# Leaving out the constant matmuls that TensorE runs inside the gaps of the norms

## The reference

```python
def _layernorm(x, g=None, b=None):
    xc = xf - jnp.mean(xf, -1, keepdims=True)
    y = xc * lax.rsqrt(jnp.mean(xc * xc, -1, keepdims=True) + NORM_EPS)

# first stack: a context stream (ctx) and a latent stream (x), two layers
#   mixer: attention + gated linear attention + 31-tap convolution, gated, times w_out
xc = _post(xc, yc, ...);  xc = _post(xc, _ffn(_modulate(xc, ...), p), ...)
x  = _post(x, _latent_mixer(...), ...);  x = _post(x, _ffn(_modulate(x, ...), p), ...)
# _ffn: (silu(h @ w_gate) * (h @ w_up)) @ w_down, inner width 2816

# second stack: latent attention, short convolution, pooling, sliding-window attention
h = rmsnorm(x, attn_norm[l]);  proj = h @ w_in[l]
gf = groups * lax.rsqrt(jnp.mean(groups * groups, axis=-1, keepdims=True) + RMS_EPS)
x = x + mixed @ w_o[l]
h2 = rmsnorm(x, ffn_norm[l])
x = x + (jax.nn.silu(gate) * up) @ w_down[l]
```

## Time and profile before

| | |
|---|---|
| runs | 3501.25, 3501.73, 3507.51 us |
| profiled execution, first to last instruction | 3497.9 us, its own time; 3.8 us under the median of the runs |
| TensorE matmul busy | 2956.0 us, 85% |
| VectorE | 2445.7 us, 70% |
| GpSimd | 2045.3 us, 58% |
| ScalarE | 1542.4 us, 44% |
| mean granted TensorE clock | 0.913 of full speed |
| DMA | 441.59 MB, mean 126 GB/s |

### The profile page before, as it was taken

One profiled execution on the slowest core, in us unless ns is written; L12 is line 12 of the kernel. 1 busy time (PEld: TensorE's weight loads), 2 busy tenths in 40 slices (PEclk: granted clock), 3 DMA queues, 4 the chain that ended last, 5 costly groups with the idle time before them and its releaser, 6 DMA issues.

```text
span 3497.9 us, 57524 instructions
## 1 busy us (share of the span) xinstructions
PE 2956.0 (85%) x21332; PEld 2740.1 (78%) x21332; DVE 2445.7 (70%) x2987; ACT 1542.4 (44%) x2508; POOL 2045.3 (58%) x823
## 2 busy tenths in 40 slices
PE   6866968889975897788998768977889989998998
PEld 5755968789974687777997756876889878997898
DVE  3978684776698858767664898676676665656565
ACT  4324544444541444434445323444354454445444
POOL 6735643658763565455874543644568545874587
PEclk7977989999987998989998979989899999999999
DMA  6424422435441343333542221322355423542354
GB/s 208 137 72 133 145 73 85 151 122 175 156 133 61 109 134 111 105 109 113 176 168 97 99 95 61 130 99 97 121 178 175 132 97 108 175 162 97 110 178 163
DMA packets 121571, 441.59 MB, mean 126 GB/s; under 512 B 13552, under 2 KB 15600, under 8 KB 120992
## 3 DMA queue, kind: packets, MB, share of 16 engines
q1 hardware_dynamic: 121088, 435.30, 37.3%
q10 hardware_dynamic: 288, 3.47, 0.2%
HBM read 437.67 MB, written 1.05 MB: 125 GB/s over the span
## 4 chain that ended last, share of the span: by engine, by line
issue 58%; POOL 38%; PE 2%; POOLq 1%; DVE 0%; ACT 0%; DVEq 0%; ACTq 0%
POOL w_lo L417 38%; PE lin L458 1%; PE lin L460 1%; PE lin L459 1%; POOLq L413 1%; POOLq L416 0%; POOLq L417 0%; DVE arena L2067 0%; DVE s_lo L1559 0%; DVE rstd L1499 0%; PE aux L565 0%; DVE rstd L1496 0%; DVE tmp L1498 0%; DVE y_buf L1597 0%; ACT w_hi L984 0%
## 5 line engine op out<-in xcount | busy, mean ns | idle before, releaser
L417 POOL TENSOR_TENSOR w_lo<-w_raw,w_hi 128x1024 fp32r<-128x1024 f32 x819 | 2045.1, 2503 | 1444.6 <-ACT w_hi L984 1440.6
L458 PE MATMUL lin<-h_hi,w_hi 128*128 128x256 f32 x3584 | 1041.0, 290 | 84.0 <-POOL w_lo L417 67.7
L459 PE MATMUL lin<-h_lo,w_hi 128*128 128x256 f32 x3584 | 1028.4, 287 | 0.0
L460 PE MATMUL lin<-h_hi,w_lo 128*128 128x256 f32 x3584 | 1027.5, 287 | 0.0
L984 ACT ACTIVATE w_hi<-w_raw 128x1024 fp32r<-128x1024 f32 x819 | 861.5, 1052 | 189.8 <-PE lin L458 113.2
L458 PEld LDWEIGHTS lin<-h_hi,w_hi 128*128 128x128 f32 x3584 | 702.7, 196 | 98.4 <-issue 64.0
L459 PEld LDWEIGHTS lin<-h_lo,w_hi 128*128 128x128 f32 x3584 | 703.2, 196 | 0.6
L460 PEld LDWEIGHTS lin<-h_hi,w_lo 128*128 128x128 f32 x3584 | 702.1, 196 | 0.0
L1621 DVE SCALAR_TENSOR_TENSOR arena<-arena,vec 128x256 f32<-128x256 f32 x720 | 517.6, 791 | 0.0
L458 PE MATMUL lin<-s_hi,w_hi 128*128 128x256 f32 x1584 | 467.4, 295 | 58.5 <-DVE s_lo L1559 23.3
L459 PE MATMUL lin<-s_lo,w_hi 128*128 128x256 f32 x1584 | 461.1, 291 | 0.0
(11 more groups left out here) (241 smaller groups left out, 4372.5 us busy)
## 6 DMA issues: line engine op xcount, KB each, us to landing
w_raw<-in_stream SPq DMA_DIRECT2D x819, 512.0 KB, 3.3
X<-in_tokens SPq DMA_DIRECT2D x2, 1024.0 KB, 10.5
arena<-in_const ACTq DMA_DIRECT2D x1, 1856.0 KB, 7.8
arena<-in_small ACTq DMA_DIRECT2D x1, 1536.0 KB, 11.2
out<-arena SPq DMA_DIRECT2D x1, 1024.0 KB, 3.9
arena<-in_masks SPq DMA_DIRECT2D x1, 960.0 KB, 12.0
const<-in_const SPq DMA_DIRECT2D x1, 690.0 KB, 7.3
wglr<-in_w_glr SPq DMA_DIRECT2D x1, 384.0 KB, 9.7
```

The costliest lines, as they stand in the source:

```text
L417: pool.tensor_tensor(w_lo[:, s, :], w_raw[:, s, :], w_hi[:, s, :].bitcast(F32), ALU.subtract).then_inc(sems["lo_ready"], 1)
L458: used(pe.matmul(o, whi, hi[:, k, :], start=k == 0, stop=False), first)
L459: pe.matmul(o, whi, lo[:, k, :], start=False, stop=False)
L460: mm = pe.matmul(o, wlo, hi[:, k, :], start=False, stop=k == kcs - 1)
```

## The change

The function, its constant and its five calls are removed. Nothing else is added or moved.

```diff
-IDLE = 10
...
-            def keep_clock(k):
-                for _ in range(k):
-                    pe.matmul(aux[3][:, 0:S], c1("mean1024"), const1[:, 0:S], start=True, stop=True)
...
                     layernorm(x, "x_ready")
                     unit(l, s, ("adt", beside[1][1]))
-                    keep_clock(IDLE)
                     n.up("h_ready", KC)
                     feed_forward()
                     if turn == 3:
                         pe.wait_ge(sems["sum_ready"], n.at("sum_ready"))
                         sum_to_mean()
                         variance(M)
-                        keep_clock(IDLE)
...
             for l in range(DEPTH):
                 variance(M)
-                keep_clock(IDLE)
                 ready = "h_ready", n.at("h_ready")
                 n.up("h_ready", KC)
                 dense_together(2, ready)
...
                 head_rows([("head256", c // 2, M[:, c, :]) for c in range(KC)])
-                keep_clock(IDLE // 2)
                 pe.wait_ge(sems["row_ready"], at.up("row_ready"))
...
                 variance(M)
-                keep_clock(IDLE)
                 n.up("h_ready", KC)
                 feed_forward()
```

## The result

The changed kernel takes 3517.16 us (median of five, 3510.05 to 3517.40) against 3501.25 us before (five, 3499.26 to 3507.51): 15.9 us slower, ratio 1.0041, interval 1.0029 to 1.0054. A second set of five runs (experiment 5) gave 3515.67 us and 1.0049 (1.0036 to 1.0063). The profiled execution has a span of 3515.4 us; 3515.9 had been worked out. The mean granted clock went from 0.913 to 0.907.

The account below looks back on a forecast made before the run. TensorE was taken to bound the long projections, so delays there count. Clock falls of 14.0 us before projections, 1.2 behind L873 and 2.8 ahead of `spread_row` summed to 18.0 us, giving 3520 us, range 3508 to 3531.

Parts of the forecast that it names:

- What bounds: Long projections: TensorE bounds, 185 of 190 us busy against GpSimd's 159 in the first feed-forward; its losses there reach the kernel.
- The removed matmuls are worth nothing: In the norm gaps, the 180 fill records, some 41 us of TensorE, are covered by the VectorE chain; removal brings 0 directly.
- A fall in every gap: Without fill, the granted clock was expected to fall in each gap of this change, 3.7 to 6.5 us long.
- 2.0 us for each of seven places: Seven places leading into projections: the half clock behind each gap costs 2.0 us, 14.0 us together; ends 8.4 and 21.
- The Trainium skill's half of the throttled time: Rule pricing a clock fall at half the throttled time: 2.6 us for a place before projections, 18 us for seven.
- L873, 1.2 us: Behind L873, the last eight `variance` records run at half clock: 1.2 us taken, 1.4 us at most, 0 at least.
- The two ahead of the spread, 1.4 each: Two places ahead of `spread_row`: the clock falls before the eight L590 records, 1.4 us each, together 2.8; ends 0 and 3.7 each.
- Sum: Whole kernel: 14.0 + 1.2 + 2.8 = 18.0 us slower, so 3515.9 us in a profile and 3520 us as median.
- (a): Rival, deep falls: the clock stays low 10 us or more at most places, +26 to +35 us, 3528 to 3537; chance 0.12.
- (b): Rival, no measurable loss: late, short falls at all seven projection places, 6 us or less, at most 3508; chance 0.09, shared.
- (c): Rival: fill at half clock ends late, so removal wins 1.6 us at such places; 3492 with all eight; chance 0.03.
- (d): Rival: the clock does not go by what TensorE does, so only noise is left, 3502; shares a chance of 0.09.

Follow-up runs that it names:

- experiment 5: The changed kernel, all ten fills out, timed again with no edit: 3515.67 us, 1.0049 against the kernel before.
- experiment 6: The kernel before with a longer fill, IDLE at 14 in place of 10: 3515.40 us, 1.0042.
- experiment 7: The kernel before with three more fill matmuls at the end of each half of a feed-forward: 3503.54 us, 1.0010.
- experiment 1: The kernel before with its fill matmuls using 16 of the array's 128 rows, same places and number: 3519.97 us, 1.0052.
- experiment 3: The kernel before with only the first stack's four fills (L866 in three passes, L873) left out: 3507.94 us, 1.0019.
- experiment 10: The kernel before with fills in eight more first-stack gaps, one shortened to four matmuls in the last pass: 3489.76 us, 0.9970.

## Why the prediction was right

- **What bounds.** Right. The feed-forwards absorbed nothing: from 745 us to the end of the first half, some 85 us later, the changed kernel keeps its delay to 0.2 us (6.8 us against before at 745, 6.6 at 834, just behind the turn), and behind the last place its 1.35 us reach the end unchanged.
- **The removed matmuls are worth nothing.** Right: the chain from reciprocal to projection is 4.96 us against 4.95.
- **A fall in every gap.** Right at the eight gaps of 4.9 to 6.5 us. At the two ahead of the spread the clock stayed at 1.00 through the gap and fell 0.8 and 1.25 us behind its end, 1.3 and 1.1 us sooner than with the fill. One sentence on the way was wrong: the unfilled gap of the earlier trace rows does not lie between the two halves of the first feed-forward but behind it, ahead of the first projections of pass 1 (L759). The price taken from it is not touched, since the code there is the same `dense_together`; the true gap between the halves is the one where the loop turns back (experiments 6 and 7), and of that I had said nothing.
- **2.0 us for each of seven places.** 12.6 us measured (2.17 + 2.27 + 1.54 + 1.80 + 2.15 + 1.34 + 1.35) for 14.0. Both unfilled gaps turned out to be models: the early fall of the earlier trace rows for passes 0 and 1 and L961 of layer 0, the late one of the earlier trace rows for L881 and L961 of layer 1; the two other places lie between. The first 48 matmuls took 7.2 to 8.4 us.
- **The Trainium skill's half of the throttled time** ("TensorE: Matmul & The Clock Gate", "HAM oscillation — how this bites in real kernels") would give 2.7 us at the first place, where 5.4 us of work ran at 0.50 (738.36 to 743.80). The records say 2.2 us; the trace is again below the rule, as it had been in the kernel before.
- **L873, 1.2 us.** 2.0 us, above the 1.4 that was to be the most. That bound took only the last eight records of `variance` as slow; fourteen of the sixteen were. **The two ahead of the spread, 1.4 each.** 1.5 us in layer 0, where the L590 records took 3.06 us (1.99 before), and 0.3 us in layer 1. The clock falls there with and without fill; what changes is only when. That last term was mis-sized the other way: 2.8 us foreseen, 1.8 us measured.
- **Sum.** 18.0 us foreseen; 16.4 us at the places, 17.5 us between the profiles, 15.9 us between the medians. That moves of +4.6, -7.0 and +3.0 us and smaller ones outside the places come to +1.1 is luck; the 16.4 at the places are not. The working had nothing for the 5.7 us won in pass 1's attention.
- **Rivals.** (a), low stretches of 10 us, came at one of ten places, ahead of the spread. (b) would have needed all seven cheap; two came near it. (c) had no place in either kernel, and appeared when the fill was made unfit (experiment 1). (d) is out by experiment 1 and by the table.

## What to carry to other kernels

Where TensorE waits some microseconds for a norm and a stretch that it bounds comes next, look at the granted clock on both sides of the wait: the price is not in the gap but in the first microseconds behind it. Matmuls that nobody reads are free there as long as they end before the data come, and as long as they use enough of the array's rows (128 held the clock here, 16 did not; nothing between was tried); a fill that is a little too long costs its overhang, one that is too short leaves the fall. Look for the gaps that have none, but do not expect a fill to cover a late return from a branch. And check a median that matters against the places: here moves of several us came and went in code that no edit had touched.

## What the runs showed of the hardware

- 16-row matmuls, back to back for 3.8 us at the pace of full ones (0.216 us from start to start), did not keep the granted clock at 1.00; 128-row ones did, in the same place (experiment 1 against the earlier trace rows).
- A gap of the same length in the same code cost 1.35 us in one profile and 2.63 in another (L961, layer 1), according to where in it the clock fell; the low stretches at the ten places lasted 3.4 to 10.2 us.
- TensorE came back from a loop's branch up to 6.2 us late with nothing to wait for that the profile names (experiment 6), and this differs from profile to profile: 0.9 us before, 2.2 in experiment 3, 2.7 in experiment 10 and 6.2 in experiment 6 at one spot. In all 50 turns without a fill, idle times of 1.7 us and more went with a 16 KB packet of the instruction queue, and those of about 1 us with none.
- VectorE records of one form, 128x256, took 0.47 us each or 2.6 us; the two long ones of pass 1's attention lay alongside GpSimd's `w_lo` (1165.15 to 1170.00), though other records alongside `w_lo` took 0.47.
